# The input projection of a decoder block as three products of high and low parts, with V turned by transposes

## The reference

```
hn   = rms_norm(x, norm_mix_g)
proj = hn @ w_in                       # 1024 x 1792
q, k, v, ga, gb = split(proj, [512, 640, 768, 1280])
q, k = rope(q), rope(k)
attn = sliding_window_attention(q, k, v, sinks)      # window 128, 8 heads on 2 KV heads
u    = ga * sigmoid(gb)
conv = silu(layer_norm(depthwise_conv_31_taps(u)))
h    = x + concat(rms_norm(attn), rms_norm(conv)) @ w_out
out  = rms_norm(h + peer_ffn(rms_norm(h)))           # queries, top-k, 16384 experts
```

## Time and profile before

| | |
|---|---|
| median of 3 runs | 2946.51 us (2942.94 to 2947.57) |
| profiled execution, its own time | 2955.07 us |
| its span | 2953.3 us |
| mean granted TensorE clock | 0.967 of full |
| busy: PE, DVE, POOL, ACT | 95%, 80%, 54%, 33% of the span |
| up to 543 us | start, projection, attention, convolution, output projection |
| from 543 us on | queries, top-k and experts |

### The profile page before, as it was taken

One profiled execution on the slowest core, in us unless ns is written; L12 is line 12 of the kernel. 1 busy time (PEld: TensorE's weight loads), 2 busy tenths in 40 slices (PEclk: granted clock), 3 DMA queues, 4 the chain that ended last, 5 costly groups with the idle time before them and its releaser, 6 DMA issues.

```text
span 2953.3 us, 33748 instructions
## 1 busy us (share of the span) xinstructions
PE 2791.9 (95%) x12016; PEld 2145.0 (73%) x12016; DVE 2357.1 (80%) x3821; ACT 976.4 (33%) x1335; POOL 1601.9 (54%) x1235
## 2 busy tenths in 40 slices
PE   7999689999799999999879999999999999999998
PEld 3546544688588888888667777777777777777776
DVE  2787943577999888898568988888888888898886
ACT  2014242311245656666222322322323223232233
POOL 1999400011012556665357777677777777777640
PEclk9999589999899999999999999999999999999999
DMA  3111010212356999999998888888888888898883
GB/s 122 36 50 40 18 43 0 79 38 85 124 165 192 316 323 342 335 341 329 340 333 300 315 301 303 311 302 305 303 302 317 294 309 307 302 318 291 313 292 141
DMA packets 253976, 685.16 MB, mean 232 GB/s; under 512 B 31984, under 2 KB 97648, under 8 KB 248432
## 3 DMA queue, kind: packets, MB, share of 16 engines
q0 software_dynamic: 104448, 335.81, 33.0%
q1 hardware_dynamic: 83568, 313.65, 29.6%
q10 hardware_dynamic: 65792, 33.56, 4.0%
HBM read 611.60 MB, written 71.30 MB: 231 GB/s over the span
## 4 chain that ended last, share of the span: by engine, by line
PE 54%; DVE 26%; DMA 10%; issue 4%; DVEq 3%; POOL 2%; ACT 2%; SPq 0%; ACTq 0%; POOLq 0%
PE ps L1627 21%; PE ps L1619 14%; DMA vring<-in_u_tab,idsA 7%; PE ps L1550 6%; DVE ps L1240 6%; DVE hnT L921 4%; PE ps L1478 3%; PE ps L1387 2%; DVE ul L1213 2%; DVE vring L1257 2%; DVE lx L1087 2%; DMA u_raw<-in_uT 2%; DVE wl L1307 1%; PE ps L1347 1%; POOL vring L542 1%
## 5 line engine op out<-in xcount | busy, mean ns | idle before, releaser
L554 POOL DMA_INDIRECT vring<-in_v_tab,idsA x512 | 553.1, 1080 | 322.1 <-DVE ps L1240 184.3
L1240 DVE SCALAR_TENSOR_TENSOR ps<-vring,hsel,ps 128x1024 f32<-128x1024 f32 x508 | 652.5, 1284 | 15.3 <-DVE ps L1240 0.5
L529 POOL DMA_INDIRECT hsel<-hidden,idsE x384 | 439.0, 1143 | 124.3 <-issue 109.5
L1627 PE MATMUL ps<-vh,wh 128*128 128x512 f32 x1024 | 402.6, 393 | 28.3 <-DVE wl L1307 28.3
L1619 PE MATMUL ps<-xh,uh 128*128 128x512 f32 x1024 | 407.6, 398 | 11.1 <-DVE ul L1213 10.4
L1627 PE MATMUL ps<-vh,wl 128*128 128x512 f32 x1024 | 405.9, 396 | 0.0
L1619 PE MATMUL ps<-xh,ul 128*128 128x512 f32 x1024 | 404.3, 395 | 0.0
L1627 PE MATMUL ps<-vl,wh 128*128 128x512 f32 x1024 | 403.7, 394 | 0.0
L1619 PE MATMUL ps<-xl,uh 128*128 128x512 f32 x1024 | 402.1, 393 | 0.0
L1592 PE MATMUL ps<-hx,xh 128*128 128x512 f32 x768 | 312.7, 407 | 41.1 <-DVE lx L1087 37.0
L859 ACT CAST vh<-v_raw 128x1024 fp32r<-128x1024 f32 x128 | 134.0, 1047 | 599.4 <-PE ps L1627 595.1
(11 more groups left out here) (188 smaller groups left out, 5011.6 us busy)
## 6 DMA issues: line engine op xcount, KB each, us to landing
xraw<-in_uX SPq DMA_DIRECT2D x128, 512.0 KB, 6.4
u_raw<-in_uT SPq DMA_DIRECT2D x128, 512.0 KB, 7.3
v_raw<-in_v_tab SPq DMA_DIRECT2D x128, 512.0 KB, 5.7
gates<-gbuf ACTq DMA_DIRECT2D x16, 2048.0 KB, 22.2
gt<-gates SPq DMA_DIRECT2D x32, 1024.0 KB, 8.2
hidden<-hst SPq DMA_DIRECT2D x93, 256.0 KB, 8.7
wqbuf<-in_w_q SPq DMA_DIRECT2D x16, 512.0 KB, 3.5
vring<-in_v_tab,idsA POOLq DMA_INDIRECT x512, 5.8
```

Of the source, the lines that this page charges most:

```text
L529: nc.gpsimd.indirect_dma_start(out=hsel[:, n, k:k + 1], out_offset=None, in_=hidden_items, in_offset=bass.IndirectOffsetOnAxis(ap=idsE[:, ...
L554: nc.gpsimd.indirect_dma_start(out=vring[q % VS][:, :], out_offset=None, in_=v_rows, in_offset=bass.IndirectOffsetOnAxis(ap=idsA[:, n, k:k ...
L1240: nc.vector.scalar_tensor_tensor(out=bank2(6), in0=vring[slot][:, :], scalar=w, in1=bank2(6), op0=ALU.mult, op1=ALU.add).then_inc(cb_done, 1)
L1627: last = mm(ps[:, 2 + k % 4, :], w[:, c, tt * P:(tt + 1) * P], v[:, c, dh * 512:(dh + 1) * 512], start=c == 0 and w is wh and v is vh, sto ...
```

## The change

Each block of the projection becomes three fp32r products for each float32 one: high weights by high hn, high by low, low by high (`project`). The high parts are copies to fp32r by ACT: of the eight slices of hn right after DVE has scaled each, into space that `acc` and the first half of `hnT` leave free; of each block of weights by `split_w`, placed by hand in ACT's program among its copies. The low parts are subtractions, in place: of hn by DVE (even k, `low_hn`) and POOL (odd k); of weights by DVE alone (`low_w`), for block 0 after the second scaling, 1 to 5 after hn, 6 after channel 1's first tap, 7 to 11 in the five rounds, between the taps and `turned`, and 12 and 13 at steps 0 and 2 of attention. TensorE waits for both parts ahead of each block. V's block is made like the others, copied to SBUF by ACT (into the last slice of `qT`), turned by eight transposes on TensorE after block 6, and copied again; DVE's last `turned` waits for that copy. SP's load of the first half of x moves behind the wait for the last half product, just ahead of `w_out`, since `hn_high` lies in its place.

```diff
+        hn_high = [at(k * 4096 if k < HT else HN + (k - HT) * 4096, f"hn_high{k}", [P, T], F32R) for k in range(DK)]
+        hn_low = at(73728, "hn_low", [P, DK, T], F32R)
+        w_low = at(106496, "w_low", [P, 4, DK, P], F32R)
+        w_high = at(16384, "w_high", [P, 4, DK, P], F32R)
...
+        def high_slot(blk):
+            return blk % 4 if blk < NCH_ALONE else blk % 4 + 2
...
+            sp.wait_ge(part_ready, 4)
             sp.dma_start(acc[:, 0:HT, :], x[0:HALF, :].rearrange("(n p) d -> p n d", p=P)).then_inc(x_in[0], 16)
-            sp.wait_ge(part_ready, 4)
             sp.dma_start(wide[:, :, :], w_out).then_inc(wout_in, 16)
...
+            for k in range(1, DK, 2):
+                pool.wait_ge(hh_ready, k + 1)
+                nc.gpsimd.tensor_tensor(hn_low[:, k, :], wide[:, k, :], hn_high[k][:, :].bitcast(F32),
+                                        ALU.subtract).then_inc(hl_odd, 1)
...
+            def split_w(blk):
+                act.wait_ge(w_in_slot[blk % 4], 16 * (blk // 4 + 1))
+                if blk >= NCH_ALONE:
+                    act.wait_ge(proj_ready, blk - 1)
+                elif blk >= 4:
+                    act.wait_ge(proj_ready, blk - 3)
+                nc.scalar.copy(w_high[:, high_slot(blk), :, :], wbuf[:, blk % 4, :, :]).then_inc(wh_in, 1)
+
+            split_w(0)
+            for k in range(DK):
+                act.wait_ge(hn_ready, k + 1)
+                nc.scalar.copy(hn_high[k][:, :], wide[:, k, :]).then_inc(hh_ready, 1)
+            for blk in range(1, 4):
+                split_w(blk)
...
             gated(0)
+            split_w(4)
             gated(1)
+            split_w(5)
+            split_w(6)
             copy_raw(0, CH_K)
+            split_w(7)
             act.wait_ge(proj_ready, CH_V + 1)
-            nc.scalar.copy(vv[:, 1:NT + 1, :].rearrange("p n d -> p (n d)"), bank2(2 * (CH_V % 2))).then_inc(v_copied, 1)
+            nc.scalar.copy(qT[:, GQ - 1, :], bank2(2 * (CH_V % 2))).then_inc(vt_copied, 1)
+            split_w(8)
             for j in range(GQ):
                 copy_raw(1 + j, CH_Q + j)
+                if j == 0:
+                    act.wait_ge(vt_turned, 1)
+                    nc.scalar.copy(vv[:, 1:NT + 1, :].rearrange("p n d -> p (n d)"), bank2(6)).then_inc(v_copied, 1)
+                if CH_Q + j + 3 < NCH_ALONE:
+                    split_w(CH_Q + j + 3)
             gated(2)
+            for blk in range(NCH_ALONE, NCH):
+                split_w(blk)
...
+            def low_w(blk):
+                dve.wait_ge(wh_in, blk + 1)
+                nc.vector.tensor_tensor(w_low[:, blk % 4, :, :], wbuf[:, blk % 4, :, :],
+                                        w_high[:, high_slot(blk), :, :].bitcast(F32), ALU.subtract).then_inc(wl_in, 1)
+
+            def low_hn(k):
+                dve.wait_ge(hh_ready, k + 1)
+                nc.vector.tensor_tensor(hn_low[:, k, :], wide[:, k, :], hn_high[k][:, :].bitcast(F32),
+                                        ALU.subtract).then_inc(hl_even, 1)
+
             for k in range(DK):
                 nc.vector.scalar_tensor_tensor(out=wide[:, k, :], in0=wide[:, k, :], scalar=par[:, G_MIX + k:G_MIX + k + 1],
                                                in1=rb[:, :], op0=ALU.mult, op1=ALU.mult).then_inc(hn_ready, 1)
+                if k == 1:
+                    low_w(0)
+                if k % 2 and k >= 3:
+                    low_hn(k - 3)
+            low_hn(DK - 2)
+            for blk in range(1, 6):
+                low_w(blk)
...
             gate_values(1)
             first_tap(1)
+            low_w(6)
...
                 if r == 0:
                     dve.wait_ge(rope_in, 16)
+                low_w(7 + r)
+                if r == GQ:
+                    dve.wait_ge(v_copied, 1)
                 turned(r)
...
                 if s < NS:
                     soft(s)
+                if s in (0, 2):
+                    low_w(NCH_ALONE + s // 2)
...
+            def project(bank, blk, k, t0):
+                high, low = w_high[:, high_slot(blk), k, :], w_low[:, blk % 4, k, :]
+                mm(bank, high, hn_high[k][:, t0:t0 + HALF], start=k == 0, stop=False)
+                mm(bank, high, hn_low[:, k, t0:t0 + HALF], start=False, stop=False)
+                return mm(bank, low, hn_high[k][:, t0:t0 + HALF], start=False, stop=k == DK - 1)
...
-                    pe.wait_ge(v_copied, 1)
+                    pe.wait_ge(vt_copied, 1)
...
-                w = wbuf[:, blk % 4, :, :]
-                if blk == CH_V:
-                    for n in range(NT):
-                        for k in range(DK):
-                            last = mm(ps[:, 2 + n // 4, (n % 4) * P:(n % 4 + 1) * P], wide[:, k, n * P:(n + 1) * P],
-                                      w[:, k, :], start=k == 0, stop=k == DK - 1)
-                else:
...
+                pe.wait_ge(wh_in, blk + 1)
+                pe.wait_ge(wl_in, blk + 1)
+                for k in range(DK):
+                    if blk == 0:
+                        pe.wait_ge(hh_ready, k + 1)
+                        pe.wait_ge(hl_odd if k % 2 else hl_even, k // 2 + 1)
+                    for hb in range(2):
+                        last = project(ps[:, 2 * (blk % 2) + hb, :], blk, k, hb * HALF)
                 last.then_inc(proj_ready, 1)
                 if blk == CH_V:
                     rotate(0)
+                if blk == CH_Q:
+                    pe.wait_ge(vt_copied, 1)
+                    for n in range(NT):
+                        last = nc.tensor.transpose(ps[:, 6 + n // 4, (n % 4) * P:(n % 4 + 1) * P],
+                                                   qT[:, GQ - 1, n * P:(n + 1) * P], ident)
+                    last.then_inc(vt_turned, 1)
...
-                    last = mm(ps[:, 7, :], wbuf[:, blk % 4, k, :], wide[:, k, j % 2 * HALF:(j % 2 + 1) * HALF],
-                              start=k == 0, stop=k == DK - 1)
+                    last = project(ps[:, 7, :], blk, k, j % 2 * HALF)
```

More of the change, by code:

```diff
@@ L306, in decoder_block @@
         pads_ready, sq_ready, sq_used, rms_root, hn_ready = sems("pads_ready sq_ready sq_used rms_root hn_ready")
+        hh_ready, hl_even, hl_odd, wh_in, wl_in, vt_copied, vt_turned = sems(
+            "hh_ready hl_even hl_odd wh_in wl_in vt_copied vt_turned")
         proj_ready = sem("proj_ready")
@@ L1361, in rotate @@
                 last.then_inc(rot_ready, 1)
+            def project(bank, blk, k, t0):
[3 more added lines that the diff above has]
+                return mm(bank, low, hn_high[k][:, t0:t0 + HALF], start=False, stop=k == DK - 1)
             pe.wait_ge(rms_root, 1)
             for blk in range(NCH_ALONE):
-                pe.wait_ge(w_in_slot[blk % 4], 16 * (blk // 4 + 1))
                 back = blk - 2
@@ L1372, in _ @@
                 elif back == CH_V:
-                    pe.wait_ge(v_copied, 1)
+                    pe.wait_ge(vt_copied, 1)
                 elif back >= CH_Q:
                     pe.wait_ge(raw_ready, back - CH_Q + 2)
-                w = wbuf[:, blk % 4, :, :]
-                if blk == CH_V:
-                    for n in range(NT):
-                        for k in range(DK):
-                            last = mm(ps[:, 2 + n // 4, (n % 4) * P:(n % 4 + 1) * P], wide[:, k, n * P:(n + 1) * P],
-                                      w[:, k, :], start=k == 0, stop=k == DK - 1)
-                else:
-                    for k in range(DK):
-                        if blk == 0:
-                            pe.wait_ge(hn_ready, k + 1)
-                        for hb in range(2):
-                            last = mm(ps[:, 2 * (blk % 2) + hb, :], w[:, k, :], wide[:, k, hb * 512:(hb + 1) * 512],
-                                      start=k == 0, stop=k == DK - 1)
+                pe.wait_ge(wh_in, blk + 1)
[6 more added lines that the diff above has]
+                        last = project(ps[:, 2 * (blk % 2) + hb, :], blk, k, hb * HALF)
                 last.then_inc(proj_ready, 1)
```

## The result

The changed kernel takes 2962.81 us (median of 6 runs, 2960.42 to 2965.71), the kernel before 2946.07 us (6 runs beside them): a ratio of 1.0059, 95% interval 1.0048 to 1.007, or 16.7 us more (interval 14.1 to 20.6). On a second chip it was 2958.47 against 2944.48, 1.0047 (1.0033 to 1.0062), 14.0 us more (9.7 to 18.3). Forecast were 2964 and 17.7 us more.

A forecast was written before the change was run, and what follows sets the result against it. TensorE bounds the first four blocks, the last and attention; DVE bounds 90.8 to 194 us. Stage end +20.2 us (including first block -1.1, subtractions +18.7), attention -2.5: +17.7 on median 2946.51, 2964 us; 8-in-10 range 2950 to 2979.

The forecast's parts named there:

- own signs of being wrong: Subtractions taking 1.2 us, first block ending before 50 or after 59 us, or the clock low through whole blocks.
- Products: TensorE's projection blocks take 11.2 us in place of 13.90, half products 2.8 in place of 3.63.
- The first block: DVE's thirteen operations end at 51 us, block at 54 (49 to 59); DVE's first subtraction at 89.7, gain 1.1 us.
- The seven subtractions: DVE's weight subtractions for blocks 5 to 11, on the chain: 2.67 us each, 18.7 us later, bounds 8.5 and 23.
- rival (a): DVE, 85 to 202 us: subtractions slip between POOL's operations, seven cost 8.5 us; total 2943 us; chance 0.15.
- the rhythm of twelve taps: Price for each DVE weight subtraction: twelve two-operand taps take 32.06 us, so 2.67 us each.
- strict turns: DVE and POOL alternating on the shared ports: 3.1 us for each subtraction, 21.6 us in place of 18.7; not used.
- The end of the stage: Block 11's sigmoid ends at 231.3 us, 20.2 us later; TensorE idles some 10, 19, 6, 6 us before blocks 7 to 10.
- Attention: Steps' half products get shorter: 5 us taken, 2.5 given back to POOL's second channel; gain 2.5 us, bounds 0 and 6.7.
- Behind the sum over channels: Everything from 382 us on is one chain behind that point and moves along with it.
- (b): TensorE's clock stays low: blocks 10 and 11 at 1.2 GHz, sum +35.5 us, 2982 us; chance 0.13.
- (c): In TensorE's products, fp32r parts cost as much as full ones: +33.7 us, 2980 us; chance 0.02.

The follow-up runs named there:

- by removal: Changed kernel without DVE's weight subtractions of blocks 5 to 11, the third product taking the high weights; ratio to the kernel before 1.0033.
- by addition to the kernel before: Kernel before with seven 128x1024 subtractions added at the same places of DVE's program, result unused; ratio to the kernel before 1.0022.
- subtractions ahead: Changed kernel with the weight subtractions for blocks 7 to 11 placed earlier among DVE's taps; ratio to the kernel before 1.0068.
- kernel with POOL cut: Changed kernel with POOL's second channel cut to its first 11 taps, the other 20 left out; ratio to the kernel before 0.9987.
- idle subtractions: Kernel before with seven 128x1024 subtractions, result unused, while DVE waits for its first gate; ratio to the kernel before 1.0001.
- V turned: Kernel before with V's block as float32 products like the others, copied, turned by eight transposes and copied again; ratio 1.0.
- x moved: Kernel before with SP's load of the first half of x behind the wait for the last half product; ratio 1.0011.

## Why the prediction was right, and which terms were not

The forecast (slower, by the sum; 2964 us) met the time, and so did the main line of its mechanism: DVE's subtractions on the chain, TensorE unable to use its gain. The terms of the sum fit less well than the total, which was met partly by luck: 17.7 us were forecast up to the output projection, 11.2 are there in the traces. Two of the prediction's own signs of being wrong came close or came true: four of the seven subtractions took 1.2 us, and the first block ended at 59.1 us (58.3 from the same start).

**Products.** Right: 10.88 us a block (11.2 forecast), the half products' steps 7.49 us in place of 8.16 (7.4 forecast).

**The first block.** Mis-sized, and not where the sum had its doubt. DVE's thirteen operations end at 52.79 us, 51.95 from the same start as before (51 forecast): POOL held DVE up by 5.9 us, a little more than the half of 9.4 that was taken. The block ended at 58.3 us from the same start and not at 54, since TensorE needed 6.3 us behind DVE's last subtraction and not 2.8:

```profile
50.44 2.35 DVE L952 TENSOR_TENSOR hn_low<-wide,hn_high 128x1024 fp32r<-128x1024 f32 x2
```

```profile
51.80 0.47 PE L1431 MATMUL ps<-hn_high,w_high 128*128 128x512 f32 x1 [2.70 <-DVE hn_low L952]
...
52.98 0.63 PE L1432 MATMUL ps<-hn_low,w_high 128*128 128x512 f32 x1
```

DVE makes the low parts of slices 4 and 6 last, one behind the other. So TensorE could take slice 4 only at 51.80 us, and four slices (24 products, some 5.5 us) were left where the sum had two. And it had waited 2.70 us: from 52.6 to 55.5 us its products start 0.43 us apart in place of 0.23, the low level, which cost 1.6 us more. With both, DVE reached its first subtraction at 93.76 us (92.9 from the same start), not 89.7.

The rule of the Trainium skill weighed there (SBUF — State Buffer, "SBUF: two separate sides") has the pair of ports locked for a whole instruction. This trace is near it: two scalings take 4.57 to 4.61 us beside one of POOL's subtractions and 2.48 without, 2.1 us more for a POOL operation of 2.36 us. Three of POOL's four fell among DVE's thirteen operations, the fourth among the weights' subtractions behind them (5.68 us for three, 3.49 without POOL).

**The seven subtractions.** Mis-sized: 18.7 us forecast, 9.9 measured (118.72 less 108.85 us), by removal 9.4, by addition to the kernel before 7.2. This is close to the price of rival (a), 8.5. The trace shows that the rhythm of twelve taps was the wrong row:

```profile
93.76 1.97 DVE L947 TENSOR_TENSOR w_low<-wbuf,w_high 128x1024 fp32r<-128x1024 f32 x1 [19.56 <-ACT w_high L624]
...
100.54 3.42 DVE L947 TENSOR_TENSOR w_low<-wbuf,w_high 128x1024 fp32r<-128x1024 f32 x1
...
164.09 1.21 DVE L947 TENSOR_TENSOR w_low<-wbuf,w_high 128x1024 fp32r<-128x1024 f32 x1
165.23 2.05 DVE L992 TENSOR_TENSOR qT<-tmp,rope 128x1024 f32<-128x1024 f32 x1
...
168.49 2.12 DVE L996 TENSOR_TENSOR qT<-qT,tmp 128x1024 f32<-128x1024 f32 x1
170.70 10.68 DVE L981 SCALAR_TENSOR_TENSOR hnT<-ubuf,par,hnT 128x1024 f32<-128x1024 f32 x4
...
210.61 1.95 DVE L947 TENSOR_TENSOR w_low<-wbuf,w_high 128x1024 fp32r<-128x1024 f32 x1
212.48 3.39 DVE L992 TENSOR_TENSOR qT<-tmp,rope 128x1024 f32<-128x1024 f32 x1
```

Beside the earlier trace rows: in round 1 the subtraction itself takes 1.21 us, the rotation's first product 2.05 in place of 1.21, its last addition 2.12 in place of 3.27. A round from its last tap to the next is 6.61 us where it was 5.78 to 5.80; in round 0, where it was 8.02, it became shorter by 1.4 us. The operation more fills time that the next one would have lost waiting for POOL. Ahead of the gate and behind the first tap it costs what I took (1.9 us and 1.2 more for the gate, then 3.4). In the last round, with the same neighbours as in rounds 1 to 3, it costs 1.9 us up to the last rotation and 1.5 more in it (3.39 for its first product, 1.94 before). So the price is not set by the neighbours alone; that it is the phase to POOL's operations fits the rows and was not tested by itself.

The rule of the Trainium skill (SBUF — State Buffer, "SBUF: two separate sides"), with strict turns, gives 21.6 us and is further off than the row of taps. The rotation's product from PSUM took 1.21 us everywhere; that it gives POOL a turn which costs DVE nothing is argued from the rows, no run took the PSUM operand away.

**The end of the stage.** Forecast +20.2 us at the sigmoid, measured 226.09 less 211.05 less the 0.84 us of the start, +14.2: 3.2 us more from the first block, 8.8 less from the subtractions, 0.5 less behind the last rotation (13.6 us to the sigmoid's end, 14.1 forecast). TensorE waited for less than forecast ahead of blocks 8 to 10, and those waits cost little (subtractions ahead). The last subtraction was not what held block 11 up: it was ready at 212.56 us, and TensorE came to block 11 only some 1.5 us later, behind block 10 (12.5 us, 13.7 forecast) and the rotation. Against the kernel before, DVE starts 2.2 us later, the subtractions add 9.9 us, the way from the last rotation to the sigmoid 2.2 us, and attention gives back 2.7: 11.5 us at the sum over channels, 11.2 at the queries.

**Attention.** Forecast -2.5, measured -2.7 (sigmoid to sum over channels, 172.5 to 169.8). Both halves were larger: 6.6 us up to the last gate (5 forecast), 3.9 given back (2.5 forecast). The kernel with POOL cut shows what POOL's work there costs. POOL's second channel starts when its first has ended, not with the sigmoid:

```profile
225.31 2.35 POOL L514 TENSOR_TENSOR hnT<-hnT,tap 128x1024 f32<-128x1024 f32 x1
227.84 2.00 POOL L506 TENSOR_TENSOR ubuf<-ubuf,hnT 128x1024 f32<-128x1024 f32 x1 [0.18 <-issue]
```

The first channel's last addition ends at 227.66 us, 1.6 us behind the sigmoid. That second bound was not in the prediction; it is why edits that bring the sigmoid 12.4 and 5.5 us forward gain 9.4 and 3.6.

**Behind the sum over channels.** Forecast: "one chain behind it and moves along". Up to the queries the change costs 11.2 and 11.5 us in its two profiles; the medians say 16.7 and 14.0. Of every kernel with three products the median is 2.5 to 5.5 us more above that of before than its profile is at the queries (on the chip with 3057 us 8 to 10). Of kernels without these products it is 0.1 us more with idle subtractions and 1.1 with V turned, but 6.3 with seven subtractions and 6.2 with x moved, so it is no mark of the three products.

From the first product of the queries to the end of the span the profiles of the changed kernel took 2408.8 and 2399.6 us, the others with three products 2399.4 to 2402.0 (without the chip with 3057 us); the kernel before took 2410.2, its three variants 2400.7 to 2403.9. So the traces show no cost of the change there. The groups of experts took 1490.2 and 1490.3 us in the profiles of the kernel before and of the idle subtractions, 1495.5 and 1493.9 in those of the change, 1491.3 to 1492.0 with the others of its kind, but also 1493.8 and 1492.0 with x moved and V turned alone, and the stage of the hidden values scatters from 695.6 to 710.0 between executions.

On the second chip the 11.2 us lie within the interval of the medians (9.7 to 18.3), on the first they lie below it (14.1 to 20.6). What the 3 to 6 us more in the medians are, and whether the change causes them, stays open. So the total was met partly by luck: the part forecast was 6.5 us too large, and 3 to 6 us that no trace places made up for it.

**Rivals.** (a), the cheap subtractions, was nearly right in the price (9.9 us, 8.5 in it) and wrong in the outcome: it had DVE start at 84.7 us (92.9 from the same start) and the sigmoid 12.3 us behind block 11's low part, where 13.6 us lay behind the last rotation's start. (b) fell: the granted clock in the stage was 0.89, low for the first 3 to 4 us of blocks 7 to 10 alone. (c) fell: a block took 10.88 us in place of 13.90.

## What to carry to other kernels

A cheaper operation on an engine that does not decide, paid for with an operation on the one that does, loses: here 9.9 us on DVE's chain; count first on whose chain the new operation stands, and behind which item of its program it makes others wait. Where two engines hold each other up, as DVE and POOL do here, price an added operation by a trial in the old kernel and not by the mean of a row of like ones, and do not expect a short job to end sooner when it is split between the two. Read from the program in which order the parts come that the next engine waits for: here two slices came ready together and last. An edit that brings one bound forward needs a look at the next: here POOL's second channel began 1 to 2 us behind the sigmoid in both kernels.

## What was not expected of the hardware

One subtraction added to a DVE program that alternates with POOL can shorten the stretch it stands in (round 0: 8.02 to 6.61 us). Four subtractions of 128x1024 given to POOL made the first block end 5.9 us later than with all eight on DVE (59.13 and 53.22 us), though DVE had four operations fewer. From the gate of the last channel on, POOL's work cost DVE 0.39 us for each us.
